# High and low activations in one 512-column product for the first 62 U tiles, with the router's casts and the seams between stages rearranged

## The chip, the cores and the metric

The kernel runs on one core of a Trainium2 chip. The metric is device time in microseconds (us) of one execution. The profile is one execution of the same program, recorded by the hardware profiler.

## The reference

The function is one decoder layer on 256 tokens of width 1024: a token mixer, then a PEER channel mixer (product-key experts). Only the second touches the change. Cut to what matters:

```
def peer(xn, wq, subkeys, u, v):            # one chunk of 128 tokens
    q = (xc @ wq).reshape(128, 8, 2, 128)
    sc = einsum('thpd,pkd->thpk', q, subkeys)        # 8 heads, 2 sides, 128 keys
    sv, si = top_k(sc, 16)                            # best 16 keys of each side
    cand = sv[:, :, 0, :, None] + sv[:, :, 1, None, :]
    cv, ci = top_k(cand.reshape(128, 8, 256), 16)     # best 16 of the 256 pairs
    i1 = take(si[:, :, 0], ci // 16); i2 = take(si[:, :, 1], ci % 16)
    g = softmax(cv)
    act = gelu(einsum('td,thkd->thk', xc, u[i1 * 128 + i2]))
    return einsum('thk,thkd->td', g * act, v[i1 * 128 + i2])
```

The kernel does not gather rows of U and V. It multiplies the tokens by all 16384 rows of U, applies gelu, weights each result by the router's gate (zero where an expert was not chosen) and multiplies by all rows of V.

## The kernel before, in words

**Numbers as two halves.** A float32 weight tile (128 partitions x 1024, 512 KB) is loaded by SyncE into one of four buffers `raw`. ScalarE rounds it to the reduced format that TensorE multiplies (`hi`, `loop_hi`, L1043 to L1047), and VectorE subtracts to get the remainder (`lo`, `loop_lo`, L1493 to L1497). There are three buffers each for `hi` and `lo` (`SPLIT`). The activations are split likewise into `xhi` and `xlo`. A product is the sum of three: high by high, high weights by low x, low weights by high x.

**Stages.** After the token mixer the query stage (16 tiles) ends about 281 us. Then come 128 U tiles (`u_tile`, L712), 8 slices of the contraction each, 3 matmuls of 256 columns a slice, accumulated in half of a PSUM bank. ScalarE applies gelu to two tiles at once (`gelu_pair`, L1049) and writes `big`. During the first 62 tiles (`ROUTER`) VectorE also runs the router. From about 471 us on each tile is preceded by a gate group (`g_group`, L728, four matmuls). The 128 V tiles (`v_tile`, L763, 12 matmuls of 512 columns) follow from about 684 us, the first half with gate groups as well.

**The router on VectorE, in program order.** It works in three parts. The key part, `choose_keys` (L1531), takes the top 16 of two rows of 128 scores, 16 times; seven of these (`EARLY`) lie in the query stage, mixed with copies of the scores out of PSUM (`sc_out`, L1476). The pair part (L1547 to L1561) has 8 rounds, each the top 16 of two rows of 256 sums that GpSimd made (L1726), then shifts and masks to get the two positions, then casts to float. The number part (L1572 to L1583) has 16 rounds: two comparisons, GpSimd's two multiplications (L1734), two reductions. Softmax and the transposes by TensorE (L748) close it.

**Order of the splits.** The order is written out by hand. `spread(upto)` (L1525) issues low halves until tile `upto` has its turn: `TILES_KEYS` (14) of them go into the key part, `TILES_PAIRS` (25) into the pair part, `TILES_NUMBERS` (21) into the number part, 60 in all. The call for tile t makes the low half of tile t+3, which needs the high half of t+3, and this needs a free buffer, hence the end of tile t on TensorE. TensorE in turn starts tile t+3 only with its low half (`loop_need`, L708). VectorE, ScalarE and GpSimd each work through their instructions in order, so a wait holds up everything behind it.

**The two seams.** At the first (about 459 to 475 us) VectorE copies the transposed router results out of PSUM, makes `gw2`, `same` and `oneA` (`keys_equal`, `rows_a`) and the gate groups begin. At the second (about 683 to 690 us) U ends and V begins: ScalarE has `loop_hi`, `gelu_pair`, `w_hi`, `squares_b`, `relu_b` (L1125, L1126 and L1139 to L1142), VectorE `group_step(0, 0, NGRP)` (L1668).

## Time and profile before

| what | value |
|---|---|
| three runs | 1070.49, 1071.54, 1076.95 us; median 1071.54 |
| profiled execution | 1069.82 us, span 1068.0 us |
| TensorE busy / VectorE busy / ScalarE busy / GpSimd busy | 1052.9 / 875.0 / 692.1 / 323.6 us |
| granted TensorE clock, mean | 0.999 |

The span goes from the first to the last instruction. Busy time counts an engine as busy while an instruction is in it; instructions overlap a little, so the time that one takes from its neighbours (from its start to the start of the next) is shorter than its own duration. PE is TensorE, DVE VectorE, ACT ScalarE, POOL GpSimd.

### The profile page before, as it was taken

The numbers are of one execution on the slowest core, as the hardware profiler recorded it, in microseconds if no ns is written. First come the engines' busy times: TensorE is split into PE (matmuls) and PEld (weight loads), VectorE is DVE, ScalarE is ACT, GpSimd is POOL, SyncE is SP. The second block draws the span as 40 slices with busy tenths as digits, with TensorE's granted clock in tenths as the row PEclk, the third lists the DMA queues.
The fourth block names the chain that finished last, engine by engine and source line by source line (L and its number), as shares of the span: only waits on it lengthen the run. The fifth ranks groups of instructions, "written<-read, shape, count | busy, mean of one in ns | idle before, by whom it ended". The sixth has DMA issues, their size and how long they took to land.

```text
span 1068.0 us, 22282 instructions
## 1 busy us (share of the span) xinstructions
PE 1052.9 (99%) x7176; PEld 955.8 (89%) x7176; DVE 875.0 (82%) x1690; ACT 692.1 (65%) x1230; POOL 323.6 (30%) x278
## 2 busy tenths in 40 slices
PE   8999999999999999999999999999999999999998
PEld 6697988989999999999999999888888888888887
DVE  5677786779999988989999999999999995444444
ACT  5365776664444444467777777899999995455543
POOL 0000210007001115633333333234444444544453
PEclk9999999999999999999999999999999999999999
DMA  6753333654455555544444444454544555555553
GB/s 252 272 189 118 111 99 102 195 189 166 141 181 188 180 186 187 179 150 160 161 158 158 158 157 157 140 176 158 166 168 158 168 204 178 197 196 190 188 195 114
DMA packets 50017, 181.36 MB, mean 170 GB/s; under 512 B 5552, under 2 KB 5680, under 8 KB 49968
## 3 DMA queue, kind: packets, MB, share of 16 engines
q1 hardware_dynamic: 49968, 180.74, 51.3%
q8 instruction: 27, 0.44, 0.2%
q14 instruction: 22, 0.18, 0.1%
HBM read 178.62 MB, written 2.10 MB: 169 GB/s over the span
## 4 chain that ended last, share of the span: by engine, by line
PE 89%; DVE 7%; ACT 2%; DMA 1%; issue 1%; POOL 0%; SPq 0%; ACTq 0%; POOLq 0%; DVEq 0%
PE bank L778 33%; PE bank L723 10%; PE bank L725 10%; PE bank L724 10%; PE bank L737 5%; PE bank L346 4%; PE bank L348 4%; PE bank L347 3%; DVE lo L1496 2%; PE bank L664 2%; PE bank L360 1%; PE bank L361 1%; PE bank L362 1%; PE bank L640 1%; PE bank L642 1%; PE bank L641 1%
## 5 line engine op out<-in xcount | busy, mean ns | idle before, releaser
L1047 ACT ACTIVATE hi<-raw 128x1024 fp32r<-128x1024 f32 x253 | 268.0, 1060 | 245.5 <-PE bank L725 151.8
L1496 DVE TENSOR_TENSOR lo<-raw,hi 128x1024 fp32r<-128x1024 f32 x253 | 315.3, 1251 | 104.8 <-ACT hi L1047 104.0
L723 PE MATMUL bank<-xhi,hi 128*128 128x256 f32 x1024 | 293.5, 287 | 0.8 <-DVE lo L1496 0.8
L725 PE MATMUL bank<-xhi,lo 128*128 128x256 f32 x1024 | 290.0, 283 | 0.0
L724 PE MATMUL bank<-xlo,hi 128*128 128x256 f32 x1024 | 289.7, 283 | 0.0
L1756 POOL TENSOR_TENSOR auxl<-big,auxh 128x256 fp32r<-128x256 f32 x126 | 168.9, 1341 | 199.4 <-ACT auxh L1083 199.4
L723 PEld LDWEIGHTS bank<-xhi,hi 128*128 128x128 f32 x1024 | 196.5, 192 | 2.2 <-issue 1.1
L724 PEld LDWEIGHTS bank<-xlo,hi 128*128 128x128 f32 x1024 | 196.3, 192 | 0.0
L725 PEld LDWEIGHTS bank<-xhi,lo 128*128 128x128 f32 x1024 | 196.0, 191 | 0.0
L778 PE MATMUL bank<-hi,auxh 128*128 128x512 f32 x508 | 160.4, 397 | 0.5 <-POOL auxl L1756 0.3
L778 PE MATMUL bank<-lo,auxh 128*128 128x512 f32 x508 | 157.2, 391 | 0.0
L778 PE MATMUL bank<-hi,auxl 128*128 128x512 f32 x508 | 156.9, 390 | 0.0
L1171 DVE TENSOR_TENSOR lo<-raw,hi 128x1024 fp32r<-128x1024 f32 x73 | 91.0, 1259 | 36.6 <-ACT hi L814 35.9
L814 ACT ACTIVATE hi<-raw 128x1024 fp32r<-128x1024 f32 x73 | 77.0, 1057 | 62.4 <-PE bank L348 32.5
L778 PEld LDWEIGHTS bank<-hi,auxl 128*128 128x128 f32 x508 | 95.4, 188 | 20.6
L778 PEld LDWEIGHTS bank<-lo,auxh 128*128 128x128 f32 x508 | 95.3, 188 | 20.2
L1743 POOL TENSOR_TENSOR oneB<-kep,eT 128x512 fp32r<-128x512 f32 x64 | 66.7, 1043 | 150.9 <-PE bank L737 141.1
L778 PEld LDWEIGHTS bank<-hi,auxh 128*128 128x128 f32 x508 | 90.6, 189 | 16.6 <-POOL auxl L1756 0.8
L1626 DVE TENSOR_REDUCE gsum<-bank 128x256 f32<-128x512 f32 x128 | 87.6, 685 | 6.9 <-PE bank L737 1.5
L1617 DVE TENSOR_TENSOR oneA<-same,gw 128x512 fp32r<-128x512 f32 x128 | 87.2, 682 | 0.0
L1077 ACT ACTIVATE oneB<-oneB 128x512 fp32r<-128x512 f32 x128 | 80.0, 625 | 2.1
L1070 ACT ACTIVATE oneB<-kep,eT 128x128 fp32r<-128x128 f32 x256 | 80.9, 387 | 0.0
(273 smaller groups left out, 1700.3 us busy)
## 6 DMA issues: line engine op xcount, KB each, us to landing
raw<-u_d SPq DMA_DIRECT2D x128, 512.0 KB, 3.4
raw<-v_d SPq DMA_DIRECT2D x128, 512.0 KB, 3.3
raw<-wpre_d SPq DMA_DIRECT2D x78, 512.0 KB, 4.0
big<-x_d SPq DMA_DIRECT2D x2, 512.0 KB, 3.7
out_d<-big SPq DMA_DIRECT2D x2, 512.0 KB, 5.3
big<-out_d SPq DMA_DIRECT2D x2, 512.0 KB, 5.0
out_d<-big SPq DMA_DIRECT2D x4, 256.0 KB, 2.1
big<-cst_d SPq DMA_DIRECT2D x1, 735.5 KB, 10.3
```

The source lines that it names most:

```text
L723: pe.matmul(out, wh, xhi[:, k, :], start=(k == 0), stop=False)
L724: pe.matmul(out, wh, xlo[:, k, :], start=False, stop=False)
L725: m = pe.matmul(out, wl, xhi[:, k, :], start=False, stop=(k == KT - 1))
L778: m = pe.matmul(bank[2 * b + f][:, :], a_, w_[:, s, f * 512:(f + 1) * 512], start=(first and st_ == 0), stop=False, skip_group_check=True)
L1047: act.activation(hi[:, slot(n), :], raw[:, n % RING, :], ACT.Copy).then_inc(hi_done, 1)
L1070: m = act.activation(oneB[:, g % 2, t, :], iota, ACT.Square, bias=i2, scale=-1.0)
L1077: act.activation(oneB[:, g % 2, :, :], oneB[:, g % 2, :, :].bitcast(F32), ACT.Relu, bias=1.0, scale=-1.0).then_inc(S("oneB_ready"), 1)
L1171: dve.tensor_tensor(lo[:, slot(n), :], raw[:, n % RING, :], hi[:, slot(n), :].bitcast(F32), ALU.subtract).then_inc(lo_done, 1)
L1496: dve.tensor_tensor(lo[:, slot(n), :], raw[:, n % RING, :], hi[:, slot(n), :].bitcast(F32), ALU.subtract).then_inc(lo_done, 1)
L1617: dve.tensor_tensor(oneA[:, g % 2, :, :, :], eq_, w_.unsqueeze(3).broadcast_to([P, 4, 2, HALF]), ALU.mult).then_inc(S("oneA_ready"), 1)
L1626: dve.tensor_reduce(gsum[:, :, :], parts, AXX, ALU.add).then_inc(S("bank67_read"), 1)
L1756: pool.tensor_tensor(auxl[:, s * T:(s + 1) * T], big[:, bass.ds(i * (UNROLL * T) + b * T, T)], auxh[:, s * T:(s + 1) * T].bitcast(F32), AL ...
```

## The change

The constants, buffers and instruction order change as shown. `u_tile_wide` replaces `u_tile` for tiles 0 to 61: for each of the 8 slices one matmul of 512 columns multiplies the high weights by high and low x side by side, and one of 256 columns adds low weights by high x into the first half of the bank. Each tile takes a whole PSUM bank, six banks in turn. ScalarE copies the second half of the bank to `big` (`low_copy`), VectorE adds the first half to it (`u_sum`), ScalarE applies gelu in place four tiles behind (`gelu_sums`, `LAG`). The scores are copied out of PSUM by ScalarE. Key positions and pair positions stay integers where they are made and are cast in bulk, and the mask and shift are written in place. `spread` now also issues `u_sum`, and its shares are 20, 21 and 19. Tiles 62 to 127 are computed as before. At both seams the order on ScalarE and VectorE differs.

```diff
@@ -65,7 +65,8 @@
 EARLY = 7
-TILES_KEYS, TILES_PAIRS = 14, 25
+LAG = 4
+TILES_KEYS, TILES_PAIRS = 20, 21
 TILES_NUMBERS = ROUTER - 2 - TILES_KEYS - TILES_PAIRS
@@ -98,13 +99,14 @@
         u_bank = (bank[4], bank[5], bank[3])
+        wide_bank = (bank[4], bank[5], bank[3], bank[0], bank[1], bank[2])
...
         lo = sb("lo", [P, SPLIT, 1024], F32R)
-        xhi = sb("xhi", [P, 8, T], F32R)
-        xlo = sb("xlo", [P, 8, T], F32R)
+        x_both = sb("x_both", [P, 8, 2, T], F32R)
+        xhi, xlo = x_both[:, :, 0, :], x_both[:, :, 1, :]
         auxh = sb("auxh", [P, SPLIT * T], F32R)
@@ -206,7 +208,7 @@
         eqt = [[carve(256) for _ in range(2)] for _ in range(2)]
-        sti, sta, stb = ([carve(16).bitcast(U32) for _ in range(2)] for _ in range(3))
+        pair_at = carve(256).bitcast(U32)
         smx = carve(32)
@@ -717,7 +719,7 @@
                 s = slot(n)
-                out = u_bank[pair % 3][:, ((base + j) % 2) * T:((base + j) % 2 + 1) * T]
+                out = u_bank[(pair + 1) % 3][:, ((base + j) % 2) * T:((base + j) % 2 + 1) * T]
                 for k in range(KT):
@@ -725,6 +727,23 @@
+            def u_tile_wide(i, j):
+                n, out = N_PRE + j, wide_bank[j % 6]
+                pe.wait_ge(S("u_sum"), i * UNROLL + (j + 1))
+                loop_need(i, n)
+                s = slot(n)
+                for k in range(KT):
+                    wh, wl = hi[:, s, k * P:(k + 1) * P], lo[:, s, k * P:(k + 1) * P]
+                    xx = x_both[:, k, :, :].rearrange("p r t -> p (r t)")
+                    if k < KT - 1:
+                        pe.matmul(out[:, :], wh, xx, start=(k == 0), stop=False, skip_group_check=True)
+                        pe.matmul(out[:, 0:T], wl, xhi[:, k, :], start=False, stop=False, skip_group_check=True)
+                    else:
+                        pe.matmul(out[:, 0:T], wl, xhi[:, k, :], start=False, stop=False, skip_group_check=True)
+                        m = pe.matmul(out[:, :], wh, xx, start=False, stop=True, skip_group_check=True)
+                m.then_inc(tile_used, 1)
             def g_group(i, j, base):
@@ -740,7 +759,7 @@
             pe.wait_ge(S("xn_lo"), KT)
-            each_tile(pe, ROUTER, lambda i, j: u_tile(i, j, 0))
+            each_tile(pe, ROUTER, u_tile_wide)
@@ -749,8 +768,10 @@
+            pe.wait_ge(S("u_sum"), ROUTER - 5 + 6)
             for j in range(ROUTER, HALF):
                 u_tile(0, j, 0)
+            pe.wait_ge(S("u_sum"), ROUTER + 6)
@@ -1023,6 +1044,13 @@
             rstd(5, st[:, 8:10])
+            def sc_out(j):
+                act.wait_ge(S("key_scores"), j + 1)
+                dst = sc.rearrange("p (b h s k) -> p h s b k", b=2, h=8, s=2)[:, j]
+                act.activation(dst, bank[6 + j % 2][:, :].rearrange("p (s b k) -> p s b k", s=2, b=2),
+                               ACT.Copy).then_inc(S("sc_out"), 1)
             for i in range(NH):
@@ -1036,6 +1064,9 @@
                 act.activation(qst[:, i % 2, :], bank[4 + i % 2][:, :], ACT.Copy).then_inc(S("bank45_read"), 1)
+                if i:
+                    sc_out(i - 1)
+            sc_out(NH - 1)
@@ -1051,7 +1082,7 @@
                     act.activation(big[:, bass.ds(i * (UNROLL * T) + (base + j - 1) * T, 2 * T)],
-                                   u_bank[(base + j) // 2 % 3][:, :], ACT.Gelu_apprx_tanh).then_inc(S("bank45_read"), 1)
+                                   u_bank[((base + j) // 2 + 1) % 3][:, :], ACT.Gelu_apprx_tanh).then_inc(S("bank45_read"), 1)
@@ -1089,6 +1120,24 @@
+            def low_copy(i, j, base):
+                act.activation(big[:, bass.ds(i * (UNROLL * T) + (base + j) * T, T)], wide_bank[(base + j) % 6][:, T:2 * T],
+                               ACT.Copy).then_inc(S("low_copied"), 1)
+            def gelu_sums(i, j):
+                two = big[:, bass.ds(i * (UNROLL * T) + (j - 1) * T, 2 * T)]
+                act.activation(two, two, ACT.Gelu_apprx_tanh).then_inc(S("bank45_read"), 1)
+            def u_step_wide(i, j):
+                loop_hi(i, N_PRE + LAG + j + SPLIT)
+                if j % 2:
+                    act.wait_ge(S("u_sum"), i * UNROLL + (6 + j + 1))
+                low_copy(i, j, LAG)
+                if j % 2:
+                    gelu_sums(i, j)
             def u_step(i, j):
@@ -1100,7 +1149,13 @@
             act.wait_ge(S("h_saved"), 16 * TB)
-            each_tile(act, ROUTER - 2, u_step)
+            for j in range(LAG):
+                loop_hi(0, N_PRE + j + SPLIT)
+                low_copy(0, j, 0)
+            each_tile(act, ROUTER - 2 - LAG, u_step_wide)
+            act.wait_ge(S("u_sum"), ROUTER - 2 + 6)
+            for j in range(ROUTER - 2 - LAG, ROUTER - 2, 2):
+                gelu_sums(0, j + 1)
             act.preload_act_table_set(LN_EXP)
@@ -1109,10 +1164,13 @@
             for j in range(ROUTER - 2, ROUTER):
-                u_step(0, j)
+                loop_hi(0, N_PRE + j + SPLIT)
+                low_copy(0, j, 0)
             act.wait_ge(S("bank67_read"), 2)
...
             fold_b(0, 0, 0)
+            act.wait_ge(S("u_sum"), ROUTER + 6)
+            gelu_sums(0, ROUTER - 1)
             for j in range(ROUTER, HALF):
@@ -1122,8 +1180,12 @@
             w_hi_tokens(0, 1, "whi_done")
+            for b in range(1, SPLIT - 1):
+                w_hi(0, b)
+            squares_b(0, 1, NGRP)
+            relu_b(0, 1, NGRP)
+            gelu_pair(0, HALF - 1, HALF)
             loop_hi(0, N_PRE + NBLK - 1 + SPLIT)
-            gelu_pair(0, HALF - 1, HALF)
@@ -1136,10 +1198,6 @@
-            for b in range(1, SPLIT - 1):
-                w_hi(0, b)
-            squares_b(0, 1, NGRP)
-            relu_b(0, 1, NGRP)
             each_tile(act, HALF - SPLIT, v_step_g)
@@ -1471,24 +1529,15 @@
             norm_x(1)
-            dve.tensor_copy(rs2, st[:, 8:10])
-            def sc_out(j):
-                dve.wait_ge(S("key_scores"), j + 1)
-                dst = sc.rearrange("p (b h s k) -> p h s b k", b=2, h=8, s=2)[:, j]
-                dve.tensor_copy(dst, bank[6 + j % 2][:, :].rearrange("p (s b k) -> p s b k", s=2, b=2)).then_inc(S("sc_out"), 1)
+            dve.tensor_copy(rs2, st[:, 8:10]).then_inc(S("u_sum"), 6)
...
                     split_lo(T_WQ + 2 * i + 4)
-                    if i:
-                        sc_out(i - 1)
-                        if i <= EARLY:
-                            dve.wait_ge(S("sc_out"), i)
-                            choose_keys(i - 1)
-                sc_out(NH - 1)
+                    if 1 <= i <= EARLY:
+                        dve.wait_ge(S("sc_out"), i)
+                        choose_keys(i - 1)
@@ -1508,17 +1557,22 @@
-                ops = [lambda c=c, s_=s_, v_=v_: dve.max(v_[:, 0:8], s_) for c, (s_, v_) in enumerate(pair)]
-                ops += [lambda c=c, s_=s_, v_=v_: dve.max_index(sti[c][:, 0:8], v_[:, 0:8], s_)
-                        for c, (s_, v_) in enumerate(pair)]
+                ops = [lambda s_=s_, v_=v_: dve.max(v_[:, 0:8], s_) for s_, v_, _ in pair]
+                ops += [lambda s_=s_, v_=v_, i_=i_: dve.max_index(i_[:, 0:8], v_[:, 0:8], s_) for s_, v_, i_ in pair]
                 ops += [lambda c=c, s_=s_, v_=v_: dve.match_replace(stg2[c][:, 0:w_], v_[:, 0:8], s_, -3e38)
-                        for c, (s_, v_) in enumerate(pair)]
-                ops += [lambda c=c, v_=v_: dve.max(v_[:, 8:16], stg2[c][:, 0:w_]) for c, (s_, v_) in enumerate(pair)]
-                ops += [lambda c=c, v_=v_: dve.max_index(sti[c][:, 8:16], v_[:, 8:16], stg2[c][:, 0:w_])
-                        for c, (s_, v_) in enumerate(pair)]
+                        for c, (s_, v_, _) in enumerate(pair)]
+                ops += [lambda c=c, v_=v_: dve.max(v_[:, 8:16], stg2[c][:, 0:w_]) for c, (_, v_, _) in enumerate(pair)]
+                ops += [lambda c=c, v_=v_, i_=i_: dve.max_index(i_[:, 8:16], v_[:, 8:16], stg2[c][:, 0:w_])
+                        for c, (_, v_, i_) in enumerate(pair)]
                 return ops
...
+            def u_sum(t):
+                dve.wait_ge(S("low_copied"), t + 1)
+                e = big[:, t * T:(t + 1) * T]
+                dve.tensor_tensor(e, wide_bank[t % 6][:, 0:T], e, ALU.add).then_inc(S("u_sum"), 1)
@@ -1526,14 +1580,14 @@
                     loop_lo(0, N_PRE + nxt_tile[0] + SPLIT)
+                    u_sum(nxt_tile[0])
                     nxt_tile[0] += 1
...
                 k2 = [slice((2 * c + p_) * 16, (2 * c + p_ + 1) * 16) for p_ in range(2)]
-                ops = top16([(sc[:, (2 * c + p_) * P:(2 * c + p_ + 1) * P], tkv[:, k2[p_]]) for p_ in range(2)], P)
-                ops += [lambda p_=p_: dve.tensor_copy(tki[:, k2[p_]], sti[p_]) for p_ in range(2)]
-                chains(ops)
+                chains(top16([(sc[:, (2 * c + p_) * P:(2 * c + p_ + 1) * P], tkv[:, k2[p_]], tki.bitcast(U32)[:, k2[p_]])
+                              for p_ in range(2)], P))
@@ -1548,17 +1602,16 @@
                 dve.wait_ge(S("pair_sums"), c + 2)
-                chains(top16([(stg[cc[x] % 4], cval[:, c16[x]]) for x in range(2)], 256))
-                spread(TILES_KEYS + (TILES_PAIRS * (c + 1)) // 16)
+                chains(top16([(stg[cc[x] % 4], cval[:, c16[x]], pair_at[:, c16[x]]) for x in range(2)], 256))
                 for x in range(2):
-                    dve.tensor_scalar(sta[x], sti[x], 4, None, ALU.logical_shift_right).then_inc(S("pairs_chosen"), 1)
-                    m = dve.tensor_scalar(stb[x], sti[x], 15, None, ALU.bitwise_and)
-                link(m)
-                for x in range(2):
-                    dve.tensor_copy(caf[:, c16[x]], sta[x])
-                    m = dve.tensor_copy(cbf[:, c16[x]], stb[x])
-                link(m)
+                    dve.tensor_scalar(caf.bitcast(U32)[:, c16[x]], pair_at[:, c16[x]], 4, None,
+                                      ALU.logical_shift_right).then_inc(S("pairs_chosen"), 1)
                 spread(TILES_KEYS + (TILES_PAIRS * (c + 2)) // 16)
+            dve.wait_ge(S("pairs_chosen"), 16)
+            link(dve.tensor_scalar(cbf.bitcast(U32), pair_at, 15, None, ALU.bitwise_and))
+            dve.tensor_copy(caf, caf.bitcast(U32))
+            dve.tensor_copy(cbf, cbf.bitcast(U32))
+            link(dve.tensor_copy(tki, tki.bitcast(U32)))
@@ -1589,7 +1642,6 @@
             dve.tensor_tensor(g3, g3, smx[:, 16:32].unsqueeze(2).broadcast_to([P, 16, 16]), ALU.mult).then_inc(S("router"), 1)
-            spread(ROUTER)
             dve.wait_ge(S("routerT"), 1)
@@ -1633,11 +1685,13 @@
+            spread(ROUTER - 1)
+            keys_equal(0, 0, 0)
+            keys_equal(0, 1, 0)
             dve.wait_ge(S("gw2_hi"), 1)
             link(dve.tensor_tensor(gw2[:, :, 1], eT[:, 2, :], gw2[:, :, 0].bitcast(F32), ALU.subtract))
-            keys_equal(0, 0, 0)
-            keys_equal(0, 1, 0)
             rows_a(0, 0, 0)
+            spread(ROUTER)
             keys_equal(0, 2, 0)
@@ -1659,13 +1713,18 @@
             each_tile(dve, NGRP - 4, u_step_g)
-            for j in range(NGRP - 4, NGRP):
+            for j in range(NGRP - 4, NGRP - 1):
                 u_step_g(0, j)
+            group_step(0, NGRP - 1, 0)
...
             V0 = N_PRE + NBLK
+            add_parts(0, 0, NGRP)
+            keys_equal(0, 0, NGRP + 3)
             dve.wait_ge(S("bank45_read"), NH + NBLK // 2)
-            group_step(0, 0, NGRP)
+            weigh(0, 0, NGRP)
+            rows_a(0, 0, NGRP + 2)
+            loop_lo(0, N_PRE + NBLK - 1 + SPLIT)
```

## Rows read from the trace of the kernel before

**Rows 1.** The page, part 1, engines: busy time, share of the span, instructions.

```profile
PE 1052.9 (99%) x7176; PEld 955.8 (89%) x7176; DVE 875.0 (82%) x1690; ACT 692.1 (65%) x1230; POOL 323.6 (30%) x278
```

**Rows 2.** Windows: length; PE, PEld, DVE, ACT, POOL busy (instructions); clock; DMA share, GB/s.

```profile
288.46:324.69 36.23, 36.23 (x299) 35.83 (x299) 35.96 (x159) 15.62 (x18) 0.00 (x0) 1.00 0.54 175
326.15:393.99 67.84, 67.09 (x550) 66.08 (x550) 67.05 (x214) 29.40 (x34) 8.46 (x14) 1.00 0.54 173
398.33:458.81 60.48, 60.48 (x507) 60.48 (x506) 52.94 (x82) 28.26 (x33) 38.62 (x32) 1.00 0.55 180
471.00:676.00 205.00, 205.00 (x1730) 205.00 (x1730) 204.90 (x309) 151.60 (x217) 64.50 (x62) 1.00 0.48 157
```

**Rows 3.** Timeline, ScalarE: start, duration, instruction, idle before and releaser; high halves.

```profile
283.93 1.06 ACT L1047 ACTIVATE hi<-raw 128x1024 fp32r<-128x1024 f32 x1 [2.82 <-PE bank L725]
...
456.58 1.06 ACT L1047 ACTIVATE hi<-raw 128x1024 fp32r<-128x1024 f32 x1 [1.82 <-PE bank L725]
```

**Rows 4.** Timeline, TensorE: a slice of a U tile, then V matmuls.

```profile
324.66 0.28 PE L723 MATMUL bank<-xhi,hi 128*128 128x256 f32 x1
324.78 0.28 PE L724 MATMUL bank<-xlo,hi 128*128 128x256 f32 x1
...
904.59 0.61 PE L778 MATMUL bank<-lo,auxh 128*128 128x512 f32 x2
905.04 0.62 PE L778 MATMUL bank<-hi,auxl 128*128 128x512 f32 x2
```

**Rows 5.** Timeline, VectorE: one round of the key part.

```profile
310.96 0.48 DVE L1511 MAX8 big<-big 128x8 f32<-128x128 f32 x2
...
313.31 0.29 DVE L1535 CAST big<-big 128x16 f32<-128x16 uint32 x2
313.64 1.23 DVE L1496 TENSOR_TENSOR lo<-raw,hi 128x1024 fp32r<-128x1024 f32 x1
```

**Rows 6.** Timeline, VectorE: end of the key part and one pair round.

```profile
326.15 0.75 DVE L1511 MAX8 big<-big 128x8 f32<-128x256 f32 x2 [1.32 <-POOL big L1726]
...
343.81 0.75 DVE L1511 MAX8 big<-big 128x8 f32<-128x256 f32 x2
...
347.61 1.23 DVE L1496 TENSOR_TENSOR lo<-raw,hi 128x1024 fp32r<-128x1024 f32 x1
348.75 0.17 DVE L1554 TENSOR_SCALAR big<-big 128x16 uint32<-128x16 uint32 x1
...
350.37 2.36 DVE L1496 TENSOR_TENSOR lo<-raw,hi 128x1024 fp32r<-128x1024 f32 x2
```

**Rows 7.** Timeline, VectorE: a number round, the end of the part, softmax.

```profile
447.29 0.74 DVE L1570 TENSOR_REDUCE big<-big 128x16 f32<-128x256 f32 x2
448.06 0.76 DVE L1576 TENSOR_TENSOR big<-kep,big 128x256 f32<-128x256 f32 x2
...
458.81 1.39 DVE L1570 TENSOR_REDUCE big<-big 128x16 f32<-128x256 f32 x4
462.17 0.42 DVE L1591 TENSOR_TENSOR big<-big 128x256 f32<-128x256 f32 x1
```

**Rows 8.** Groups by line and form: low halves between 397 and 459 us; ScalarE copies.

```profile
L1496 DVE TENSOR_TENSOR lo<-raw,hi 128x1024 fp32r<-128x1024 f32 x22 | 33.7, 1530 | 8.6 <-ACT hi L1047 8.6
...
L941 ACT ACTIVATE big<-bank 128x256 f32<-128x256 f32 x16 | 6.1, 383 | 6.8 <-PE bank L348 6.4
```

**Rows 9.** Timeline, VectorE: four additions from PSUM at the end of the mixer.

```profile
221.85 2.48 DVE L1468 TENSOR_TENSOR big<-big,bank 128x512 f32<-128x512 f32 x4
```

**Rows 10.** Timeline, TensorE: first seam and second seam.

```profile
462.65 0.88 PE L748 MATMUL bank<-kep,big 128*128 128x128 f32 x6 [0.35 <-DVE big L1591]
463.28 0.36 PE L723 MATMUL bank<-xhi,hi 128*128 128x256 f32 x1
...
470.66 0.66 PE L737 MATMUL bank<-oneA,oneB 128*128 128x128 f32 x4 [1.39 <-DVE oneA L1617]
...
688.62 0.63 PE L737 MATMUL bank<-oneA,oneB 128*128 128x128 f32 x4 [1.39 <-issue]
```

## The prediction

> **What bounds the kernel now.** I read the engines' busy time first: TensorE is busy for 1052.9 of 1068.0 us, VectorE for 875.0 [rows 1]. An average does not say which of the two sets the pace where the change acts, so I read busy time by stretch next. In the key part VectorE is busy for 35.96 of 36.23 us, in the pair part for 67.05 of 67.84, in the number part for 52.94 of 60.48 [rows 2]. TensorE is shown as busy nearly throughout, but ends of matmuls are modelled, so I check its pace instead. A slice takes three steps of 0.120 us [rows 4], a tile 24 x 0.120 = 2.88 us. ScalarE makes a high half when a tile ends: at 283.93 us for tile 0, at 456.58 us for tile 59 [rows 3]. That is 172.65 us for 59 tiles, which need 169.9. TensorE therefore loses 2.7 us, although its row says it is busy. Both engines are within 2% of being the bound here, VectorE in the key and pair parts, TensorE in the number part. The change takes work from TensorE and gives VectorE more, so the sum that matters is VectorE's.
>
> **TensorE's side.** A 512-column matmul takes 0.45 / 2 = 0.225 us from start to start, a 256-column one 0.120 [rows 4]. The new tile is 8 x (0.225 + 0.120) = 2.76 us, 0.12 less. Over 62 tiles that is 7.4 us; with the 2.7 us of late low halves 10.1 us could go, if nothing else held it. The Trainium skill's page "TensorE: Matmul & The Clock Gate", section "Back-to-back issue gap", gives the spacing of isolated matmuls as N / 2.4 GHz plus 2.5 ns, by which merging two products would save only 2.5 ns, 0.02 us a tile and 1.2 us over 62. The row of 256 columns is 13 ns above N / 2.4 GHz, so here the trace speaks for the larger saving.
>
> **VectorE's side: what is added.** `u_sum`, one a tile, 256 elements with one operand in PSUM. Four such additions of 512 occupy 2.48 us, 0.62 each [rows 9]; two reductions of 256 follow one another at (448.06 - 447.29) / 2 = 0.38 us, the last four take 1.39, 0.35 each [rows 7]. I take 0.34 us, near the fastest 256-element rows; the bounds are 0.31 (half of 0.62) and 0.42 (a whole duration). A low half takes 348.75 - 347.61 = 1.14 us of VectorE [rows 6], so a tile now costs 1.48.
>
> **What is removed.** In each key round two casts, 313.64 - 313.31 = 0.33 us [rows 5], leaving 313.31 - 310.96 = 2.35. In each pair round the shifts, masks and casts took 350.37 - 348.75 = 1.62 us; two shifts stay, 0.17 together. The 8 copies of the scores go to ScalarE, which has time: it is busy for 15.62 of 36.23 us [rows 2]. Four bulk instructions come between pair and number part: 3 of 256 elements and one of 512, taken as 1.7 us (0.35 each, 0.6 for the long one, two waits of 0.05); bounds 0.7 and 2.4.
>
> **The new sequence.** I follow VectorE to X, the moment when it is done with the 60th tile; before, X is 458.81 us [rows 7].
> - Key part. Nine rounds and 20 tiles are 9 x 2.35 + 20 x 1.48 = 50.8 us of work. It begins about 283 us (288.46 less a low half of 1.14, a key round of 2.68 with casts, two copies of 512 elements from PSUM at about 0.6 [rows 9] and casts of 0.33) and could end at 334. But the call for tile 19 waits for TensorE to finish tile 19: 283.93 + 19 x 2.76 + 0.2 for the loop = 336.6, then 1.0 for the high half and 1.48: 339.1. Five us of VectorE's time are lost in waits, because 20 tiles are asked for where TensorE is not that far yet.
> - Pair part. The first sums of GpSimd cost 1.4 us (1.32 idle [rows 6]): 340.5. Eight rounds of (347.61 - 343.81) + 0.17 = 3.97 [rows 6] are 31.8, 21 tiles are 31.1: 403.4. GpSimd's sums used to run beside the casts and now fall beside low halves. In the number part, where GpSimd works beside them, a low half takes 1.530 us against 1.23 [rows 8, 6]. So between 0 and 21 x 0.30 = 6.3 us come on top; I take 1.2, since VectorE's shift is followed at once by a low half that can start before GpSimd does: 404.6.
> - Number part. Bulk casts: 406.3. Sixteen pairs of comparisons at about 0.69, fourteen pairs of reductions at 0.77 [rows 7], 19 tiles at 1.48: 49.9. The slowing of low halves recurs, 22 x 0.30 = 6.6 us [rows 8]. X = 462.8, 4.0 us later than before.
>
> From 340.5 to X VectorE spends 122.3 us on 40 tiles, 3.06 a tile, against TensorE's 2.76. The bound changes hands: TensorE waits in the pair part for low halves behind a 3.80 us chain, about 1 us in most rounds, and then again for the router. Whether `u_sum` itself is slowed beside GpSimd no row shows. The reductions beside it are not (0.38), so I take nothing, and 16 x 0.3 = 4.8 us as the upper bound. The Trainium skill's page "SBUF — State Buffer", section "Who interferes with whom", says that a VectorE instruction with at most one SBUF input does not contend with GpSimd; no row here shows it for an addition from PSUM.
>
> **ScalarE.** `low_copy` is 0.38 us [rows 8] a tile, hidden: it fits in the idle before a high half, 1.82 us at the last [rows 3]. If that cover were gone, high halves would come late. `gelu_sums` waits for a sum four tiles back, which VectorE needed to pass anyway. Two gelus of 512 elements now stand between the last sum and the table load ahead of the exponential. At 0.38 us for 256 elements [rows 8] they are at most 1.5 us; I take 0.6 as visible (bounds 0 and 1.5). SyncE's loads wait for low halves as before; a load has two tiles, over 5 us, before its high half is due, so nothing is added.
>
> **First seam.** Before, X to the first gate group is 470.66 - 458.81 = 11.85 us, with 1.39 idle on TensorE [rows 7, 10]. Now: 3.78 to the router's end (462.17 + 0.42 - 458.81), 0.6 for the gelus, 0.05, 0.63 for the transposes (462.65 to 463.28 [rows 10]), two plain tiles 5.76: 10.8. VectorE's chain in those tiles (copies, one low half, comparisons, `gw2`, `rows_a`) is about as long. TensorE's new wait for all sums before tile 64 stands behind `rows_a` and a low half: 0.5. Net -0.5 us (bounds -1.0 and +1.0).
>
> **Second seam.** TensorE idles 1.39 us before the second gate group of V [rows 10]. ScalarE now does its squares before the high half and the gelu, so this group is ready earlier, but the high half of the third V tile comes some 2 us later, just in time. I take -1.0 (bounds -1.4 and +0.5).
>
> **Sum.** 4.0 - 0.5 - 1.0 = +2.5 us on the profiled execution's 1069.8: 1072.3. The median of the runs is 1.7 us above that execution, on which basis it is 1074.0. I forecast 1073.5. From 471 us on TensorE is busy for 205.00 of 205.00 us and the U tiles are the old ones [rows 2], so everything there shifts along.
>
> **Rivals.**
> - *VectorE's contention does not recur* (faster by a little). With sums between the low halves GpSimd may find free slots; of 7.8 us that I set, up to all go, X = 455.0, total -5.3: 1065 to 1067. Against it: GpSimd needs the same 32 multiplications in less idle time. Chance 0.20.
> - *TensorE stays the bound* (faster by over 1%). Then tile 61 ends at 283.93 + 61 x 2.76 + 0.8 = 453.1 instead of 462.3, and with the idle times of both seams it is about -12: 1058. It decides if VectorE serves a tile in 2.76 us; my sum says 3.06. Chance 0.03.
> - *VectorE's queue is longer still* (slower). Sums at 0.42 (+4.8 over 60), slowed beside GpSimd (+4.8), low halves beside the pair sums (+5.1): together +15, with the forecast's own +2.5 1087; one of them alone 1077 to 1079. The place is the pair and number parts, and 13 us of extra work before X put it over 1%, less what I have counted, so 8 us more than my sum. Chance 0.12, of which 0.03 over 1%.
> - *TensorE's clock falls* (slower). It was granted 1.00, 2.4 GHz, in all these stretches [rows 2], with hardly a pause. Now it pauses about 1 us in most pair rounds and 3 to 4 us before the router ends. At 1.2 GHz a tile would take twice 2.76; from four such tiles on the loss passes 11 us: 1084. Chance 0.02.
> - *Merging saves almost nothing on TensorE.* If a tile took 2.86, the key part would end 1.9 us later and all that follows: 1075.5. Chance 0.05.
> The forecast itself, within about -3 and +6 us, has 0.58.
>
> One per cent, 10.7 us, is about what a measurement of this kernel tells from no change. The range takes in the second and fourth cases only in their nearer parts: 1066 to 1080. Faster by over 1%: 0.03; slower: 0.05; within 1%: 0.92.
>
> **What would show it.** Step between matmuls in a new tile: 0.225 after the wide one, 0.12 after the narrow one. VectorE idle in the key part (about 5 us, waiting for high halves) and idle nowhere between 341 and 463 us. TensorE waiting for low halves in the pair part, and 3 us or more for the router's last product. `u_sum` near 0.42 us long. X at 463. First gate group at 474 instead of 470.66 with no idle before it, and none before the second of V. I am wrong if X comes before 459, or if TensorE does not wait there.

## The result, and the profile after

The change made the kernel slower: 1078.51 us median of 6 runs (1077.3 to 1080.17) against 1071.14 us for before, 6 runs on the same chip. The ratio is 1.007, 95% interval 1.0059 to 1.0081. The forecast was 1073.5, with a range of 1066 to 1080. The measured time lies 1.5 us inside the upper end of that range: the sign was as forecast, but the loss was +7.4 us, not +2.5. The profiled execution took 1080.17 us. Page, span and engines (beside [rows 1]):

```profile
span 1078.4 us, 21399 instructions
...
PE 1052.7 (98%) x6680; PEld 930.1 (86%) x6680; DVE 879.9 (82%) x1668; ACT 713.5 (66%) x1300; POOL 338.7 (31%) x278
```

TensorE has 496 instructions fewer and is busy for the same time (the ends of matmuls are modelled, so busy time does not tell its pace). Stretches of U, in the columns of [rows 2]: key, pair and number part, then the first seam.

```profile
286.61:344.13 57.52, 57.52 (x329) 50.04 (x327) 51.54 (x181) 32.00 (x50) 1.24 (x3) 1.00 0.56 177
344.13:407.47 63.34, 58.99 (x331) 50.26 (x330) 63.06 (x186) 31.93 (x51) 20.12 (x14) 1.00 0.51 163
408.66:467.78 59.12, 56.13 (x308) 46.84 (x307) 58.63 (x98) 29.40 (x47) 40.54 (x32) 1.00 0.52 167
480.70:482.00 1.30, 1.26 (x7) 1.29 (x8) 0.63 (x2) 1.30 (x3) 0.26 (x1) 0.63 0.54 139
482.00:484.00 2.00, 2.00 (x12) 2.00 (x10) 1.96 (x2) 1.97 (x5) 0.78 (x1) 0.50 0.46 180
484.00:486.00 2.00, 2.00 (x17) 2.00 (x17) 1.90 (x4) 0.76 (x2) 0.00 (x0) 0.88 0.48 127
```

VectorE is busy nearly throughout from 344 to 468 us (63.06 of 63.34, 58.63 of 59.12), where before it had 7.5 us to spare in the number part. In the key part it idles 6 of 57.5 us. The clock column of the last three rows belongs to the first seam, below. High halves on ScalarE (beside [rows 3]):

```profile
286.61 1.06 ACT L1078 ACTIVATE hi<-raw 128x1024 fp32r<-128x1024 f32 x1 [0.97 <-PE bank L744]
...
289.40 1.06 ACT L1078 ACTIVATE hi<-raw 128x1024 fp32r<-128x1024 f32 x1 [1.47 <-PE bank L744]
...
292.22 1.06 ACT L1078 ACTIVATE hi<-raw 128x1024 fp32r<-128x1024 f32 x1 [1.49 <-PE bank L744]
...
462.23 1.06 ACT L1078 ACTIVATE hi<-raw 128x1024 fp32r<-128x1024 f32 x1 [2.14 <-PE bank L744]
```

A wide tile takes 2.82 us where TensorE alone sets the pace, and 59 tiles took 175.62 us, 3.0 longer than before. TensorE's longest waits between 281 and 486 us (engine, tile, line, who ended it, us in total, times, longest):

```profile
PE bank L740 <- DVE lo L1545: 3.8, 8, 0.9
PE bank L740 <- ACT hi L1078: 3.4, 3, 1.2
PE bank L767 <- DVE big L1644: 3.3, 1, 3.3
PE bank L756 <- DVE big L1575: 1.8, 1, 1.8
```

The last two, for the router (L767) and at the gate group (L756), were 0.35 and 1.39 us before [rows 10]. VectorE at the end of the key part and in the first pair round, beside [rows 6]:

```profile
341.19 1.23 DVE L1545 TENSOR_TENSOR lo<-raw,hi 128x1024 fp32r<-128x1024 f32 x1 [1.25 <-ACT hi L1078]
...
344.13 0.76 DVE L1560 MAX8 big<-big 128x8 f32<-128x256 f32 x2 [1.31 <-POOL big L1785]
...
348.09 1.22 DVE L1545 TENSOR_TENSOR lo<-raw,hi 128x1024 fp32r<-128x1024 f32 x1
349.23 0.42 DVE L1575 TENSOR_TENSOR big<-bank,big 128x256 f32<-128x256 f32 x1
349.56 1.31 DVE L1545 TENSOR_TENSOR lo<-raw,hi 128x1024 fp32r<-128x1024 f32 x1
```

One wait of 1.25 us for a high half at the last asked tile, then GpSimd's first sums, then per tile 1.14 of low half and 0.33 of sum. In the number part, groups of VectorE (beside [rows 8]; count, busy us, mean ns, idle):

```profile
L1545 DVE TENSOR_TENSOR lo<-raw,hi 128x1024 fp32r<-128x1024 f32 x19 | 32.5, 1710 | 0.0
...
L1575 DVE TENSOR_TENSOR big<-bank,big 128x256 f32<-128x256 f32 x19 | 7.8, 412 | 0.0
```

The end of that part and the first seam, VectorE (beside [rows 7]) and TensorE (beside [rows 10]). Between them stands one line of the kernel before, its two comparisons ahead of the gate group (`same`), which take 2.11 us now and took 1.48:

```profile
467.78 1.38 DVE L1623 TENSOR_REDUCE big<-big 128x16 f32<-128x256 f32 x4
...
475.75 2.11 DVE L1660 TENSOR_TENSOR same<-kep,eT 128x256 f32<-128x256 f32 x2
...
478.23 0.69 DVE L1669 TENSOR_TENSOR oneA<-same,gw 128x512 fp32r<-128x512 f32 x1
478.84 1.22 DVE L1545 TENSOR_TENSOR lo<-raw,hi 128x1024 fp32r<-128x1024 f32 x1
479.98 0.42 DVE L1575 TENSOR_TENSOR big<-bank,big 128x256 f32<-128x256 f32 x1
```

```profile
468.53 1.48 DVE L1608 TENSOR_TENSOR same<-kep,eT 128x256 f32<-128x256 f32 x2
```

```profile
472.31 0.87 PE L767 MATMUL bank<-kep,big 128*128 128x128 f32 x6 [3.29 <-DVE big L1644]
...
480.74 0.80 PE L756 MATMUL bank<-oneA,oneB 128*128 128x128 f32 x4 [1.80 <-DVE big L1575]
...
482.08 0.41 PE L725 MATMUL bank<-x_both,hi 128*128 128x256 f32 x1
482.29 0.41 PE L726 MATMUL bank<-x_both,hi 128*128 128x256 f32 x1
...
485.65 0.56 PE L756 MATMUL bank<-oneA,oneB 128*128 128x128 f32 x4
```

TensorE stood 3.29 us for the router and 1.80 us for the sum that starts at 479.98. Then the granted clock fell from 1.00 (2.4 GHz) to 0.50 (1.2 GHz) for 3.4 us: matmuls of 256 columns came every 0.21 us instead of 0.12. The first gate group is 4.91 us ahead of the second instead of 3.42; not all of this is the clock's, as the experiments show. The second seam, where the idle 1.39 us of [rows 10] is gone:

```profile
694.80 0.57 PE L756 MATMUL bank<-oneA,oneB 128*128 128x128 f32 x4
...
698.75 0.63 PE L756 MATMUL bank<-oneA,oneB 128*128 128x128 f32 x4
```

To compare executions I count from the first U matmul, because the stage before it ended at 280.78 us in one and at 283.46 in the other; in the seven kernels below whose code is the same up to there it lies between 280.84 and 283.84.

| stretch, us | before | after | difference |
|---|---|---|---|
| first U matmul to transposes | 181.87 | 188.85 | +7.0 |
| transposes to first gate group | 8.01 | 8.43 | +0.4 |
| first to second gate group | 3.42 | 4.91 | +1.5 |
| gate group 64 to 66 | 8.67 | 7.38 | -1.3 |

The sum is +7.6, and the medians say +7.4. "Transposes" are TensorE's six transposes of the router's results (L748 before, L767 after).

### The profile page after: what moved, and what is told of

It reads as the page before. It is cut to its first block, busy times and chain, and to the rows that moved or that the text cites. A ratio compares the mean times of both kernels' runs of the same rounds, so it can differ in the third digit from the quotient of the medians.

```text
span 1078.4 us, 21399 instructions
## 1 busy us (share of the span) xinstructions
PE 1052.7 (98%) x6680; PEld 930.1 (86%) x6680; DVE 879.9 (82%) x1668; ACT 713.5 (66%) x1300; POOL 338.7 (31%) x278
## 4 chain that ended last, share of the span: by engine, by line
PE 82%; DVE 14%; DMA 2%; ACT 2%; issue 1%; POOL 0%; SPq 0%; ACTq 0%; POOLq 0%; DVEq 0%
PE bank L799 32%; PE bank L725 6%; PE bank L727 6%; PE bank L726 6%; DVE lo L1545 5%; PE bank L756 5%; PE bank L348 4%; PE bank L350 3%; PE bank L349 3%; PE bank L740 3%; PE bank L666 2%; PE bank L741 2%; DVE big L1575 1%; DVE big L1629 1%; DMA raw<-wpre_d 1%; DVE big L1623 1%
## 5 line engine op out<-in xcount | busy, mean ns | idle before, releaser
L740 PE MATMUL bank<-x_both,hi 128*128 128x512 f32 x434 | 156.8, 400 | 7.3 <-DVE lo L1545 3.8
L725 PE MATMUL bank<-x_both,hi 128*128 128x256 f32 x528 | 153.0, 290 | 0.0
L727 PE MATMUL bank<-x_both,lo 128*128 128x256 f32 x528 | 150.2, 285 | 0.0
L726 PE MATMUL bank<-x_both,hi 128*128 128x256 f32 x528 | 150.0, 284 | 0.0
L741 PE MATMUL bank<-x_both,lo 128*128 128x256 f32 x434 | 121.7, 280 | 0.0
L740 PEld LDWEIGHTS bank<-x_both,hi 128*128 128x128 f32 x434 | 81.6, 188 | 28.6 <-issue 7.3
L725 PEld LDWEIGHTS bank<-x_both,hi 128*128 128x128 f32 x528 | 102.1, 193 | 0.0
L726 PEld LDWEIGHTS bank<-x_both,hi 128*128 128x128 f32 x528 | 101.8, 193 | 0.0
L727 PEld LDWEIGHTS bank<-x_both,lo 128*128 128x128 f32 x528 | 101.5, 192 | 0.0
```

What stands on the lines that cost most here:

```text
L725: pe.matmul(out, wh, xhi[:, k, :], start=(k == 0), stop=False)
L726: pe.matmul(out, wh, xlo[:, k, :], start=False, stop=False)
L727: m = pe.matmul(out, wl, xhi[:, k, :], start=False, stop=(k == KT - 1))
L740: pe.matmul(out[:, :], wh, xx, start=(k == 0), stop=False, skip_group_check=True)
L741: pe.matmul(out[:, 0:T], wl, xhi[:, k, :], start=False, stop=False, skip_group_check=True)
```

## The experiments

The theory after the result: VectorE sets the pace through the sums, the low halves slowed by GpSimd, and a key share too large; the rest is one wait at the first seam and the clock behind it. The rival: the wide tile, ScalarE's extra copies or the two new orders lose time themselves. Two kernels set the ends, then parts were undone one by one. Each was timed together with the kernel before on one chip; the ratio is to before. "The stretch" is the one from first U matmul to transposes. "Shares" are the tiles of key, pair and number part.

**Narrow tiles, all else kept.** Tiles 0 to 61 as before the change, no sums, shares 14/25/21; bulk casts, score copies on ScalarE and both orders stay.

```diff
-each_tile(pe, ROUTER, u_tile_wide)
+each_tile(pe, ROUTER, lambda i, j: u_tile(i, j, 0))
-TILES_KEYS, TILES_PAIRS = 20, 21
+TILES_KEYS, TILES_PAIRS = 14, 25
```

> Tiles 0 to 61 are computed as in the kernel before (three 256-column products a slice, no sum on VectorE, no copy of the low part), with its shares 14, 25 and 21; bulk casts, score copies on ScalarE and both reordered seams of the changed kernel stay. Theory A (the 60 sums on VectorE are what costs): VectorE falls back behind TensorE's pace, TensorE loses none of the 2.7 us of late low halves, the second seam keeps its 1.3 us: 1066 to 1068 us, 0.3 to 0.5% faster than before. Theory B (the reordered seams, with their new places of waits, are what costs): the first seam still loses 2 to 3 us, 1070 to 1073.

Measured: 1066.63 us (1066.24 to 1068.85), ratio 0.9962 [0.9949, 0.9975]; the stretch is 179.80 us. TensorE's and VectorE's waits, same columns as above:

```profile
PE bank L725 <- ACT hi L1076: 0.6, 1, 0.6
PE bank L767 <- DVE big L1632: 0.4, 1, 0.4
```

```profile
DVE lo L1534 <- ACT hi L1076: 14.3, 22, 1.7
```

So the wide product with its sums and shares costs 11.9 us against this kernel, and the other parts of the change gain 4. VectorE has 14.3 us of slack for high halves where the changed kernel has 3.3. The rival's "new orders" are answered here too: with both orders kept, transposes to second gate group take 6.68 + 4.18 = 10.86 us, against 11.43 before and 13.34 in the changed kernel.

**The first seam.** `u_sum` is waited for one tile earlier, and ScalarE makes the next high half ahead of its own wait.

```diff
-pe.wait_ge(S("u_sum"), ROUTER + 6)
+pe.wait_ge(S("u_sum"), ROUTER - 1 + 6)
...
+loop_hi(0, N_PRE + ROUTER + SPLIT)
 act.wait_ge(S("u_sum"), ROUTER + 6)
 gelu_sums(0, ROUTER - 1)
-for j in range(ROUTER, HALF):
-    u_step(0, j)
+u_step(0, ROUTER + 1)
```

> The changed kernel, with TensorE's wait for all sums before the first gate group lowered by one (the bank of tile 64 held tile 60), and ScalarE's high half of tile 65 put ahead of its wait for the last sum. Theory A: of the 7.4 us only those at the first seam go: the gate group starts 1.8 us earlier, and if the pause was what let TensorE's clock fall to 0.50 in 482 to 484 us, that 1.5 us goes too: 1075 to 1077. Theory B: most of the loss goes: 1071 to 1073.

Measured: 1077.51 us (1075.87 to 1077.73), ratio 1.0056 [1.0041, 1.0072], 1 us below the changed kernel by the medians and a little above what I expected. The 1.80 us wait is gone, and transposes to second gate group fell from 13.34 to 12.14 us. Part of the gain was lost to the clock, which fell anyway, now at the transposes (windows as in [rows 2]):

```profile
470.00:472.00 2.00, 1.01 (x5) 1.01 (x6) 0.87 (x3) 1.99 (x2) 0.00 (x0) 0.72 0.02 6
472.00:474.00 2.00, 2.00 (x11) 2.00 (x10) 1.39 (x3) 1.97 (x5) 0.32 (x1) 0.50 0.00 0
```

One of its four executions had a mean granted clock of 1.00 and took 1075.87 us; the other three had 0.997 to 0.998 and took 1077.37 to 1077.73. That puts the price of the fall in this kernel at about 1.5 to 1.9 us, from a single execution without it.

**The shares.** The key share back to 14, the rest of the change kept (diff as above, second part).

> The changed kernel with the shares of tiles 14, 25 and 21 instead of 20, 21 and 19, nothing else. Theory A in the form of my prediction: VectorE stood idle about 4.7 us in the key part because 20 tiles are asked for before TensorE has them, and as VectorE sets the end of the router, these come back: the router ends about 5 us earlier, 1073 to 1075. If VectorE's total work alone decides and its idle time would fall elsewhere: no change, 1077 to 1079.

Measured: 1074.74 us (1073.38 to 1076.24), ratio 1.004 [1.0025, 1.0056]; the stretch is 185.36 us, 3.5 less. VectorE's waits for high halves fell from 3.3 to 1.1 us. The 20-tile share alone costs half of the loss. In the profiled execution the clock fell here as well, right behind the transposes: it was 0.50 from 468 to 471 us.

**Both of these.**

> The changed kernel with both repairs: shares 14, 25, 21 and the two waits at the first seam moved. If the two losses are separate they add up: 3.8 and 1.0 us off 1078.5, so 1073 to 1075, still slower than before by 2 to 3 us, since the 60 sums stay. Theory B (the waits and the order are the whole loss): at or below 1071.

Measured: 1075.49 us (1073.19 to 1077.89), ratio 1.0034 [1.0022, 1.0047]: the same as the shares alone. The two edits don't add up. With the shares alone TensorE waited only 0.3 us for the sum (1.8 in the changed kernel), but transposes to first gate group took 8.43 us in both: TensorE ran its two tiles at half clock and so filled the time in which it would have waited for VectorE. Transposes to second gate group went from 12.42 to 12.14 us, so the seam edit had 0.3 us left to gain. Its profiled execution lost more than that elsewhere: the clock fell a second time, from 335 to 338 us, behind a wait of 2.33 us for a low half, and the stretch is 186.41 us against 185.36. The same wait (2.26 us) stands in the profiled execution of the shares alone, without a fall behind it.

**Sums of one element.** The 62 additions cover one element each. The other elements keep only the product of the high weights with low x, so the results are wrong, for the main part of each sum is left out; queue, semaphores and order stay.

```diff
-e = big[:, t * T:(t + 1) * T]
-dve.tensor_tensor(e, wide_bank[t % 6][:, 0:T], e, ALU.add).then_inc(S("u_sum"), 1)
+e = big[:, t * T:t * T + 1]
+dve.tensor_tensor(e, wide_bank[t % 6][:, 0:1], e, ALU.add).then_inc(S("u_sum"), 1)
```

> The changed kernel with VectorE's sum cut from 256 elements to one, all waits and the number of instructions kept; it leaves out the addition of the high part, so this is a price alone. A one-element operation takes about 0.08 us of VectorE instead of 0.34: 60 x 0.26 = 16 us less work. Theory A: VectorE is no longer the bound, the router ends at TensorE's pace (about 10 us earlier), 1067 to 1070. Theory B: 1076 to 1079.

Measured: 1071.29 us (1070.23 to 1073.5), ratio 1.0008 [0.9999, 1.0017]; 7.2 us less than changed, and short of what I expected. VectorE cannot use what it saves while the key part asks for 20 tiles:

```profile
DVE lo L1545 <- ACT hi L1078: 10.5, 12, 1.5
```

This execution also shows the first seam without a fall of the clock. TensorE, the first two gate groups and the windows there:

```profile
472.00 0.63 PE L756 MATMUL bank<-oneA,oneB 128*128 128x128 f32 x4 [1.53 <-DVE big L1575]
475.99 0.63 PE L756 MATMUL bank<-oneA,oneB 128*128 128x128 f32 x4 [0.39 <-issue]
```

```profile
472.00:476.00 4.00, 3.60 (x29) 3.43 (x29) 3.29 (x3) 3.97 (x7) 1.04 (x1) 1.00 0.43 135
```

From the first to the third gate group it is 3.99 + 3.39 = 7.38 us, and the same 7.38 in the kernels with the shares undone and with matmuls in pairs, where the clock had fallen and risen again before the first group. Before the change it is 6.74, in the changed kernel 4.91 + 3.32 = 8.23. So of the 1.5 us lost there about 0.85 is the clock; 0.64 stays at full clock, with the new order.

**The same with shares 14/25/21.**

> The sum cut to one element (the addition of the high part is left out) and the shares 14, 25, 21. With sums alone cut the kernel took 1071.3 us, 7.2 less than the changed kernel, and VectorE still waited 11.2 us for high halves, most of it in the key part. Theory A with the shares as second term: those waits move to where TensorE is the bound, the router ends 2 to 3 us earlier: 1068 to 1070. If the shares matter only while the sums are there: 1071 to 1072.

Measured: 1066.0 us (1065.0 to 1066.58), ratio 0.9948 [0.9931, 0.9964], better than expected. The stretch is 177.58 us, the shortest of all. This is what the wide product could be worth with sums for nearly nothing: 2.2 us of the stretch against narrow tiles. In the profiled execution the first seam takes it back: the wait at the gate group costs 1.5 us, and first to second group is 4.90 us against 4.18, with the clock at 0.50 from 468 to 471 us. By their ratios the two kernels can't be told apart (0.9948 and 0.9962, with overlapping intervals). The wide tile and ScalarE's extra copies are all in this kernel, so they lose no time in the stretch themselves.

**GpSimd's multiplications made small.** In the number part its 256-element products cover one sixteenth, so the selected numbers are wrong; count and order of the instructions stay.

```diff
-pool.tensor_tensor(e3, e3, tki[:, at_:at_ + 16].unsqueeze(1).broadcast_to([P, 16, 16]),
+pool.tensor_tensor(e3[:, 0:1, :], e3[:, 0:1, :], tki[:, at_:at_ + 16].unsqueeze(1).broadcast_to([P, 1, 16]),
                    ALU.mult).then_inc(S("picked"), 1)
```

> The changed kernel with GpSimd's 32 multiplications of the number part cut from 256 elements to 16; it leaves out most of picking the key numbers, so it is a price alone. In the changed kernel the 19 low halves there take 1.71 us instead of 1.23: 9.1 us. If GpSimd's overlap is the cause, they fall to 1.23 to 1.3 us, the router ends 8 to 9 us earlier and the time is 1069 to 1071. If they are slow for another reason (loads, the sums): no change, 1077 to 1079.

Measured: 1071.08 us (1070.42 to 1073.97), ratio 0.9997 [0.9987, 1.0007]; 7.4 us less than changed. Low halves of that part:

```profile
L1545 DVE TENSOR_TENSOR lo<-raw,hi 128x1024 fp32r<-128x1024 f32 x19 | 23.5, 1239 | 2.1 <-ACT hi L1078 2.1
```

The 1710 ns of the changed kernel become 1239; 19 x 0.47 = 8.9 us, of which 6.7 show in the stretch (182.13 us). Of the 0.48 us by which a low half was slowed 0.47 are GpSimd's doing. This gain and that of the one-element sums (7.2 us) are each about the whole loss, so they don't add: either one gives VectorE back its time.

**Wide and narrow matmuls in pairs.** Odd slices multiply narrow first, so that equal widths follow one another: 8 changes of width in a tile instead of 14.

```diff
-if k < KT - 1:
+if k < KT - 1 and k % 2 == 0:
```

> The changed kernel with the narrow product first in every second slice, so that two wide and two narrow ones follow each other in turn. The new tile takes 2.82 us, not the 2.76 that 8 x (0.225 + 0.120) gives. If each change of width costs about 4 ns, a tile takes 2.79 us; if the wide product itself is slower here than in the V stage, 2.82 stays.

One execution: 1076.07 us. A tile takes 2.78 to 2.79 us. Matmuls of the changed kernel (first) and of this one:

```profile
301.11 0.40 PE L740 MATMUL bank<-x_both,hi 128*128 128x512 f32 x1
301.35 0.28 PE L741 MATMUL bank<-x_both,lo 128*128 128x256 f32 x1
301.46 0.40 PE L740 MATMUL bank<-x_both,hi 128*128 128x512 f32 x1
301.71 0.28 PE L741 MATMUL bank<-x_both,lo 128*128 128x256 f32 x1
```

```profile
300.45 0.40 PE L740 MATMUL bank<-x_both,hi 128*128 128x512 f32 x1
300.69 0.28 PE L741 MATMUL bank<-x_both,lo 128*128 128x256 f32 x1
300.81 0.27 PE L743 MATMUL bank<-x_both,lo 128*128 128x256 f32 x1
300.92 0.40 PE L744 MATMUL bank<-x_both,hi 128*128 128x512 f32 x1
```

(2.82 - 2.787) / 6 = 5.5 ns for each change of width, on average. The stretch is 188.20 us against 188.85: of the 2 us that 60 shorter tiles would save, 0.65 show in a kernel that waits for VectorE.

**The parts of the change alone.** First the bulk casts and score copies on ScalarE, both seams as before:

```diff
-ops += [lambda p_=p_: dve.tensor_copy(tki[:, k2[p_]], sti[p_]) for p_ in range(2)]
+link(dve.tensor_copy(tki, tki.bitcast(U32)))
```

> The kernel before, with the positions cast in bulk and the router's scores copied by ScalarE; tiles, shares and both seams as before. The theory (VectorE's queue set the router's end before, and 60 low casts of 0.33 us taken out of its rounds shorten it, partly lost in waiting for ScalarE's high halves): the stretch from the first U product to the router's transposes 179.8-180.5 us in place of 181.87, the second seam 8.67 us as before; 1068.5-1069.5 us, ratio 0.9975-0.9985. The rival (the bulk cast and the unchanged first seam eat it): 1070.5-1071.5 us.

Measured: 1069.23 us (1068.87 to 1071.51), ratio 0.9979 [0.9969, 0.9989]; the stretch is 179.80 us, as in the kernel with narrow tiles. Then the second seam's order alone, its edit the last hunks of the change on ScalarE and VectorE:

> The kernel before, with the second seam alone in the changed order (low half of group 65 ahead of the positions' rest, relu of group 64 placed as in the changed kernel). The theory (the second seam gives about 1.3 us wherever it is put, because TensorE's idle of 1.39 us ahead of group 65 goes): from the start of gate group 64 to that of group 66 7.38 us in place of 8.67, everything ahead of it as before, 1069.5-1070.2 us, ratio 0.9985-0.999. The rival (the gain came from the other parts' state at that point, and is given back behind it): 1071 us and a ratio of 1.000.

Measured: 1069.79 us (1068.62 to 1072.23), ratio 0.9986 [0.9976, 0.9996]. Gate groups 64 and 66 on TensorE:

```profile
686.82 0.57 PE L737 MATMUL bank<-oneA,oneB 128*128 128x128 f32 x4
...
694.20 0.63 PE L737 MATMUL bank<-oneA,oneB 128*128 128x128 f32 x4
```

7.38 us from the first to the third, as expected, with no idle.

**First squares by ScalarE.** The kernel with narrow tiles, with one of GpSimd's two first distances taken over by ScalarE.

```diff
-fold_b(0, 0, 0)
+for t in range(4):
+    m = act.activation(oneB[:, 0, t, :], iota, ACT.Square, bias=eT[:, 1, t:t + 1], scale=-1.0)
...
+relu_b(0, 0, 0)
...
-distances(0, 0, 0)
```

> This kernel is e1_narrow (all 64 tiles as before the change, the pair shares 14/25/21, bulk casts of the positions, score copies on ScalarE, both seams in the changed order), with one edit: in the first gate group ScalarE makes the squares that GpSimd makes in e1_narrow as its second distance, 3.26 us long, beside which VectorE's two keys_equal took 2.45 us. The theory (what is left at the first seam is VectorE's chain slowed by that distance): the two keys_equal fall to 1.9-2.3 us, low half 64 comes up to 0.5 us earlier, G0 no later than in e1_narrow, G0 to G1 3.7-4.1 us; 1065.5-1066.6 us, ratio to before 0.995-0.996. The rival (the squares on ScalarE come ahead of the gelus that TensorE waits for, and ScalarE is as late as VectorE there): G0 to G1 4.3-4.8 us and 1066.8-1067.5 us.

Measured: 1066.72 us (1065.64 to 1067.83), ratio 0.9954 [0.9939, 0.9969]. VectorE's comparisons for the gate and low half 64, narrow tiles first, then this kernel:

```profile
464.00 2.45 DVE L1648 TENSOR_TENSOR same<-kep,eT 128x256 f32<-128x256 f32 x2
...
467.42 1.22 DVE L1534 TENSOR_TENSOR lo<-raw,hi 128x1024 fp32r<-128x1024 f32 x1
```

```profile
464.21 1.60 DVE L1651 TENSOR_TENSOR same<-kep,eT 128x256 f32<-128x256 f32 x2
...
466.79 1.22 DVE L1537 TENSOR_TENSOR lo<-raw,hi 128x1024 fp32r<-128x1024 f32 x1
```

The comparisons fell from 2.45 to 1.60 us, more than I had said. Counted from the first U matmul, low half 64 came 0.87 us earlier, and first to second gate group fell from 4.18 to 3.55 us. Against before the two kernels can't be told apart by their medians (1066.63 and 1066.72), so the 0.63 us is seen in the profile only. Both beat before and after.

## Why the prediction was right or wrong

**The mechanism was right.** VectorE became the bound from the pair part on; TensorE waited for low halves and then for the router. The kernel with narrow tiles, sums and 20-tile share gone, is 11.9 us faster; the one with all but the width of the sums is 7.2 us faster. The rival in which TensorE stays the bound fell at once.

**The 60th tile, X.** Counted from the first high half of U, X came at 467.78 - 286.61 = 181.2 us; the forecast had 462.8 - 283.93 = 178.9 and before was 174.9. So +6.3 in place of +4.0. By parts, measured against forecast: up to the pair part 57.5 against 56.6, pair part 63.3 against 64.1, casts 1.2 against 1.7, number part 59.1 against 56.5.

- *Sum, 0.34 us a tile*: right. Start to start is 0.33, the mean duration 415 ns. Beside GpSimd it stays 412 ns [the group of L1575 above]. The upper bound of 4.8 us for it was not touched. The Trainium skill's page "SBUF — State Buffer", section "Who interferes with whom", says that a VectorE instruction with at most one SBUF input, outside its two-port modes, does not contend with GpSimd. The trace agrees: 412 ns in the number part and 418 ns in the key part, where GpSimd is nearly idle (1.24 of 57.52 us).
- *Tile, 2.76 us*: mis-sized. It took 2.82, since a change of width costs time, which my rows of equal widths could not show. That makes 19 x 0.06 = 1.1 us of the later key part. By the formula that the prediction cited from the Trainium skill's page "TensorE: Matmul & The Clock Gate", section "Back-to-back issue gap", merging would save 0.02 us a tile. The trace has 0.06 saved, between the formula and my 0.12.
- *Contention in the number part, 22 x 0.30 = 6.6 us*: mis-sized, and this is the largest term. The mean of 1530 ns in [rows 8] mixed low halves beside GpSimd with free ones. Now most are beside it: 19 x (1.710 - 1.226) = 9.2 us, and the small-multiplication kernel gives back 1710 to 1239. That is the 2.6 us by which the part was too long.
- *Contention in the pair part*: right in size (1.2 us set; 21 x (1.257 - 1.226) = 0.7 measured). GpSimd started as VectorE began a low half, but only the second was slowed, 1.31 us.
- *Key part*: I saw that the 20-tile share idles VectorE and counted 5 us for it. It idled 4.7 us ahead of its low halves there, 3.3 of them waiting for high halves, and the shares kernel shows the price, 3.5 us in the stretch and 3.8 in the medians.

**First seam, -0.5 us.** This step failed: +1.9 us from transposes to second gate group, where I had a small gain from X on. From X to the first gate group it took 12.96 us, before 11.85, forecast 11.35. Up to the transposes it went as I had said (4.53 us, forecast 4.43). Then the term of 0.5 us for TensorE's wait for all sums was mis-sized: the group waited 1.80 us for a sum that was queued behind `rows_a` and a low half. I had taken VectorE's chain as about as long as TensorE's two tiles. It is longer, in part because the two comparisons now run beside GpSimd's distances: 2.11 us, against 1.48 before the change. The kernel with ScalarE's squares shows the same dependence (2.45 to 1.60). Behind the first group I had put nothing, and 1.5 us were lost: 0.64 that stay at full clock, and about 0.85 by the clock.

**Clock.** I gave it 0.02 and 11 us. It did fall, from 1.00 (2.4 GHz) to 0.50 (1.2 GHz), for 3.4 us after TensorE had been idle for 3.29 and 1.80 us, and cost 8.23 - 7.38 = 0.85 us in the profiled execution. The place was in the forecast's list of waits; the price was a fraction of what I had set, for I let it last four tiles at half speed. It fell in most of the kernels that wait at this seam, also with one-element sums and the shares undone, where TensorE waited only 1.68 and 1.54 us. It did not fall in the profiled execution of the one-element sums, where the waits were 3.02 and 1.53 us. Nor is one kernel always the same: seven of the ten executions of the one-element sums had a mean granted clock of 0.995 to 0.998 over the whole kernel, three had 1.00. So the length of the pauses alone does not tell whether it falls.

**Second seam, -1.0 us.** Right, measured -1.3, and -1.3 again in the kernel with this order alone.

**Bulk casts.** Right in direction, and I had not given them a figure of their own: together with the score copies on ScalarE they are worth 2.1 us of the stretch with narrow tiles.

The time ended 5 us above the number by three misses: X +2.3, first seam +3.1, second seam -0.3. The rival "VectorE's queue is longer still" had 1077 to 1079 for one of its three parts. The measured time lies there, but none of the three was the cause, so this agreement is luck.

Not settled: what makes the clock fall in one execution and not in another with the same waits, and whether a mix of wide and narrow tiles that fills VectorE's 14.3 us would gain. At 0.06 us a tile it is at most 0.06 x 60 = 3.6 us.

## What to carry to other kernels

Moving work from the engine that is busy to one that is nearly as busy needs a price on both sides: here 0.06 us of TensorE a tile was bought with 0.33 us of VectorE. A mean duration that mixes slowed and free instances of an instruction is not its price once the mix changes; split it by what runs beside it. The small parts of a change may be worth keeping when its main idea is not: the bulk casts with the score copies gave 2.4 us by the medians, the second seam's order 1.8, and all other parts together 4.4 with narrow tiles.

## What the runs showed of the hardware

- A change of matmul width costs about 5.5 ns (tiles of 2.82 and 2.787 us with 14 and 8 changes).
- A VectorE subtraction of two SBUF tiles (1024 elements) goes from 1226 to 1710 ns beside GpSimd's multiplications, and back to 1239 when these are small. An addition with one operand in PSUM stays at 412 ns.
- The granted clock was 0.50 for 3.4 us after TensorE pauses of 3.3 and 1.8 us, in other runs after one of 3.3 us or of 2.3 us alone and after 1.7 and 1.5 us; it stayed at 1.00 after 3.0 and 1.5 us. What a fall costs depends on where it lies: 0.85 us between the first two gate groups of the changed kernel, nothing that shows ahead of them with the shares undone, where TensorE would otherwise have waited for VectorE.
